# Second block of a transformer kernel: the index query and the small projection as two groups of 356 columns ahead of the query

## The reference, cut to what matters

```python
h = rmsnorm(x, norm_mix[layer])
proj = h @ w_in[layer]
qa, ka, va, qb, kb, vb, qi, ki, wi, ga, gb = jnp.split(proj, IN_OFFSETS, axis=-1)
...
qb = rope(qb.reshape(B, T, B_HEADS, HEAD_DIM), pos)
kb = rope(kb[:, :, None], pos)[:, :, 0]
qi = rope(qi.reshape(B, T, IDX_HEADS, IDX_DIM), pos)
ki = rope(ki[:, :, None], pos)[:, :, 0]
y_b = indexed_sparse_attention(qb, kb, vb, qi, ki, wi).reshape(B, T, D_B)
```

## Time and profile before

| what | before |
|---|---|
| median of 3 runs | 729.28 us (728.77 to 729.98) |
| the profiled execution | 728.69 us, of which the span from first to last instruction is 726.9 us |
| PE busy | 715.3 us, 98% of the span, 3776 matmuls |
| DVE, ACT, POOL busy | 515.6 us, 410.3 us, 25.0 us |
| chain that ended last | PE 90%, DVE 3%, ACT 2%, issue 2% |
| granted TensorE clock, mean | 0.999 |

### The profile page before, as it was taken

The page is one execution under the profiler, slowest core; times in us unless marked ns, Lnnn a source line. Parts: engine busy times, 40 slices in busy tenths (PEclk is TensorE's granted clock), DMA queues, the critical chain, the costliest instruction groups (busy, mean ns, idle before and its releaser), DMA issues.

```text
span 726.9 us, 9709 instructions
## 1 busy us (share of the span) xinstructions
PE 715.3 (98%) x3776; PEld 575.7 (79%) x3776; DVE 515.6 (71%) x908; ACT 410.3 (56%) x693; POOL 25.0 (3%) x44
## 2 busy tenths in 40 slices
PE   7999999999999999999999999999999999999996
PEld 5678885578888888888888777778888888888885
DVE  4689999897665866747898799766856455545544
ACT  4397658986754564456546676675465444344432
POOL 1030012001000000000100000000000000000000
PEclk9999999999999999999999999999999999999999
DMA  9994939517656576643558334443376556555511
GB/s 367 414 366 158 387 102 365 205 59 261 210 185 230 202 273 233 231 174 115 161 177 301 131 117 130 158 177 116 116 232 231 174 186 206 187 175 173 174 58 59
DMA packets 72717, 144.90 MB, mean 199 GB/s; under 512 B 4112, under 2 KB 27664, under 8 KB 71648
## 3 DMA queue, kind: packets, MB, share of 16 engines
q1 hardware_dynamic: 70864, 138.98, 54.9%
q0 software_dynamic: 1520, 5.03, 2.0%
q10 hardware_dynamic: 288, 0.27, 0.1%
HBM read 143.22 MB, written 1.05 MB: 198 GB/s over the span
## 4 chain that ended last, share of the span: by engine, by line
PE 90%; DVE 3%; ACT 2%; issue 2%; DMA 1%; POOL 0%; SPq 0%; POOLq 0%; DVEq 0%
PE bank L433 22%; PE bank L435 22%; PE bank L434 22%; PE bank L757 5%; PE bank L415 5%; PE bank L755 3%; DMA WX<-in_w_ada 1%; DVE WL L1543 1%; PE bank L509 1%; PE bank L452 1%; PE bank L473 1%; PE bank L512 1%; PE bank L515 1%; PE bank L889 1%; PE bank L911 1%
## 5 line engine op out<-in xcount | busy, mean ns | idle before, releaser
L1543 DVE TENSOR_TENSOR WL<-W,WH 128x1024 fp32r<-128x1024 f32 (+2 forms) x222 | 249.6, 1170 | 36.0 <-ACT WH L1042 35.8
L1042 ACT ACTIVATE WH<-W 128x1024 fp32r<-128x1024 f32 (+2 forms) x222 | 211.9, 1011 | 51.0 <-DMA W<-in_w_mlp 35.7
L433 PE MATMUL bank<-WH,AHL 128*128 128x512 f32 (+1 forms) x480 | 189.0, 394 | 0.7 <-DVE WL L1543 0.4
L435 PE MATMUL bank<-WH,AHL 128*128 128x512 f32 (+1 forms) x480 | 185.4, 386 | 0.0
L434 PE MATMUL bank<-WL,AHL 128*128 128x512 f32 (+1 forms) x480 | 185.2, 386 | 0.0
L433 PEld LDWEIGHTS bank<-WH,AHL 128*128 128x128 f32 x480 | 90.2, 188 | 22.1 <-issue 4.0
L435 PEld LDWEIGHTS bank<-WH,AHL 128*128 128x128 f32 x480 | 90.1, 188 | 18.6
L434 PEld LDWEIGHTS bank<-WL,AHL 128*128 128x128 f32 x480 | 90.3, 188 | 16.9
L433 PE MATMUL bank<-WH,HH 128*128 128x512 f32 (+1 forms) x218 | 84.9, 390 | 0.0
L435 PE MATMUL bank<-WH,HL 128*128 128x512 f32 (+1 forms) x218 | 84.5, 388 | 0.0
L434 PE MATMUL bank<-WL,HH 128*128 128x512 f32 (+1 forms) x218 | 84.4, 387 | 0.0
(11 more groups left out here) (276 smaller groups left out, 853.0 us busy)
## 6 DMA issues: line engine op xcount, KB each, us to landing
W<-in_w_mlp SPq DMA_DIRECT2D x32, 1024.0 KB, 5.5
W<-in_w_in SPq DMA_DIRECT2D x24, 1024.0 KB, 5.8
W<-in_w_gate SPq DMA_DIRECT2D x22, 512.0 KB, 4.0
W<-in_w_up SPq DMA_DIRECT2D x22, 512.0 KB, 5.1
W<-in_w_down SPq DMA_DIRECT2D x11, 1024.0 KB, 5.0
W<-in_w_ada SPq DMA_DIRECT2D x10, 1024.0 KB, 7.9
WX<-in_w_ada SPq DMA_DIRECT2D x10, 1024.0 KB, 10.7
W<-in_w_out SPq DMA_DIRECT2D x8, 1024.0 KB, 5.1
```

The lines of the kernel that those rows point to most:

```text
L433: e.matmul(po, hs, wh[:, k, c0:c0 + cw], start=first and k == 0, stop=False)
L435: ins = e.matmul(po, ls, wh[:, k, c0:c0 + cw], start=False, stop=last and k == unit.nk - 1)
L1042: e.activation(m.WH[unit.slot][:, c], m.W32[unit.slot][:, c], ACT.Copy).then_inc(S["w_hi"], 1)
L1543: e.tensor_tensor(m.WL[unit.slot][:, c], m.W32[unit.slot][:, c], m.WH[unit.slot][:, c].bitcast(F32), ALU.subtract).then_inc(S["w_lo"], 1)
```

## The change

It regroups the 712 columns of qi and s and puts them ahead of qb. The unit "qi" now holds the first 356 columns of qi; the unit "s" holds the other 156 columns of qi and the 200 small columns, loaded in three pieces. Both take 356 columns. The slots stay in sequence: qi has W_0 and W_1 as before, s now W_4 and W_5, qb now W_2 and W_3. In `first2` PE runs qi, s, qb, and the turn of token block 1's norm stands in the middle of qb(0) and not behind it. ACT takes s's bank out in two copies (156 columns to raw, 200 to small), and the order of ACT's copies and DVE's rotations follows. On ACT the two high halves of W_5 no longer stand together between the second and the third sum of squares: one is there, the other between the third and the fourth. The matmuls' count stays.

```diff
-    two("qi", "w_in_2", 2176, True, "qi_mm", (3, 4))
+    two("qi", "w_in_2", 2176, True, "qi_mm", (3, 4), 356)
+    for i in range(2):
+        add("s", "w_in_2", 4 * i, 4, [("w_in_2", 2532, 156), ("w_in_2", 2048, 128), ("w_in_2", 2688, 72)], True, ("s_mm", 3 + i))
     two("qb", "w_in_2", 1536, True, "p2_mm", (3, 4))
-    for i in range(2):
-        add("s", "w_in_2", 4 * i, 4, [("w_in_2", 2048, 128), ("w_in_2", 2688, 72)], True, ("s_mm", 3 + i))
...
     def first2(tb):
-        product(by["qi"], m.AH, m.AL, tb, 4 + tb, "qi_mm", n_ready(1, tb))
-        frees(4 + tb, ("p2_out", 3 * tb + 1))
-        product(by["qb"], m.AH, m.AL, tb, tb, "p2_mm", n_ready(1, tb))
-        frees(tb, ("p2_out", 3 * tb + 2))
-        if tb == 0:
-            norm_turn(3, 1)
-        product(by["s"], m.AH, m.AL, tb, 2 + tb, "s_mm", n_ready(1, tb), 200)
-        frees(2 + tb, ("p2_out", 3 * tb + 3))
+        product(by["qi"], m.AH, m.AL, tb, 4 + tb, "qi_mm", n_ready(1, tb), 356)
+        frees(4 + tb, ("p2_out", 4 * tb + 1))
+        product(by["s"], m.AH, m.AL, tb, 2 + tb, "s_mm", n_ready(1, tb), 356)
+        frees(2 + tb, ("p2_out", 4 * tb + 3))
+        product(by["qb"], m.AH, m.AL, tb, tb, "p2_mm", n_ready(1, tb), 512, None if tb else lambda: norm_turn(3, 1))
+        frees(tb, ("p2_out", 4 * tb + 4))
...
-    def between(tb, mid):
+    def between(tb):
         i = 8 + 4 * tb
+        halves = high_halves(tb)
         for n in range(2):
             for j in range(2):
                 w.wait_ge(S["btw"], 8 * tb + 3 * n + 2 + j)
                 square(i + 2 * n + j, m.X[:, tb, 512 * n:512 * n + 512], m.S1[:, tb, 512 * n:512 * n + 512])
-            hi(mid[n])
+                if n != j:
+                    next(halves, None)
+        for _ in halves:
+            pass
...
     w.wait_ge(S["m2_mm"], 64)
     hi(2)
-    raw_out(0, "qi_mm", 2, 4, 0, 1.0)
+    index_out(0)
+    small_out(0)
+    norm_features(3, 1, m.mix, None)
     raw_out(1, "p2_mm", 2, 0, 0, 0.125)
-    norm_features(3, 1, m.mix, None)
-    small_out(0)
-    raw_out(0, "qi_mm", 4, 5, 1, 1.0)
+    hi()
+    index_out(1)
+    hi()
+    small_out(1)
     hi()
     raw_out(1, "p2_mm", 4, 1, 1, 0.125)
     hi()
-    small_out(1)
-    hi(2)
...
-    projected(1, 0, 0)
-    projected(2, 1, 0)
+    projected(2, 0, 0)
     small2(0)
-    projected(3, 0, 1)
+    projected(4, 1, 0)
     lo()
-    projected(4, 1, 1)
+    projected(5, 0, 1)
     lo()
     small2(1)
     features2(2, two(m.qiT, 1))
-    lo(2)
-    projected(7, 0, 0)
-    projected(7, 0, 1)
+    lo()
+    projected(7, 1, 1)
+    lo()
+    projected(9, 0, 0)
+    projected(9, 0, 1)
```

More of the change, by code:

```diff
@@ L848, in qa @@
         product(by["qa"], m.AH, m.AL, tb, 2 + tb, "p2_mm", n_ready(1, tb), 512, between)
-        frees(2 + tb, ("p2_out", tb + 7))
+        frees(2 + tb, ("p2_out", tb + 9))
     qa(0, lambda: p2_turn(m.rr[0], 5, (("p2_act", 1), ("p2_dve", 1))))
     for i in (1, 0):
-        w.wait_ge(S["p2_r"], 8)
+        w.wait_ge(S["p2_r"], 7)
         b = turn([(tb, m.skk[i][:, tb, :]) for tb in range(2)], "p2_turned")
@@ L859, in tensor_program @@
         product(by["ka"], m.AH, m.AL, tb, tb, "p2_mm", n_ready(1, tb))
-        frees(tb, ("p2_out", tb + 9))
+        frees(tb, ("p2_out", tb + 11))
         dots(4 * tb)
@@ L866, in tensor_program @@
                 (lambda: p2_turn(m.rr[1], 12, (("p2_act", 6), ("p2_act", 7)))) if tb else None)
-        frees(2 + tb, ("p2_out", tb + 11))
+        frees(2 + tb, ("p2_out", tb + 13))
     def gate(p, half):
@@ L904, in pv2 @@
         w.wait_ge(S["pt2"], 2 * p + 2)
-        w.wait_ge(S["p2_out"], 12)
+        w.wait_ge(S["p2_out"], 14)
         take(2)
@@ L1334, in between, with index_out @@
                 square(i + 2 * n + j, m.X[:, tb, 512 * n:512 * n + 512], m.S1[:, tb, 512 * n:512 * n + 512])
-            hi(mid[n])
+                if n != j:
+                    next(halves, None)
+        for _ in halves:
+            pass
         w.wait_ge(S["rstd"], 8 + 2 * tb)
         copy(m.S1[:, tb, 512:1024], m.X[:, tb, 512:1024], "nscale_act", m.stat[:, 47 + 2 * tb:48 + 2 * tb])
-    between(0, (0, 0))
+    between(0)
     norm_features(2, 0, m.mix, None)
     hi()
-    between(1, (1, 0))
+    between(1)
+    def index_out(tb):
+        from_bank("qi_mm", 2 + 2 * tb, m.raw[0][:, tb, 0:356], 4 + tb, slice(0, 356), "p2_out")
     def small_out(tb):
-        from_bank("s_mm", 2 + 2 * tb, m.small[:, tb, :], 2 + tb, slice(0, 200), "p2_out")
+        from_bank("s_mm", 2 + 2 * tb, m.raw[0][:, tb, 356:512], 2 + tb, slice(0, 156), "p2_out")
+        from_bank("s_mm", 2 + 2 * tb, m.small[:, tb, :], 2 + tb, slice(156, 356), "p2_out")
     def raw_out(i, sem, value, bk, tb, scale):
@@ L2058, in small2 @@
     def small2(tb):
-        w.wait_ge(S["p2_out"], 3 * tb + 3)
+        w.wait_ge(S["p2_out"], 4 * tb + 3)
         for i, c0 in ((0, 0), (1, 128)):
             rope2(m.skk[i][:, tb, :], m.small[:, tb, c0:c0 + 64].unsqueeze(1).to_broadcast([128, 2, 64]), 2, tb)
-    projected(1, 0, 0)
-    projected(2, 1, 0)
+    projected(2, 0, 0)
     small2(0)
-    projected(3, 0, 1)
+    projected(4, 1, 0)
     lo()
-    projected(4, 1, 1)
+    projected(5, 0, 1)
     lo()
@@ L2091, in vector_program @@
     for tb in range(2):
-        projected(9, 1, tb)
+        projected(11, 1, tb)
     features2(8, two(m.qaT, 1))
```

## The result

The change is slower: its median is 732.79 us (4 runs, 731.92 to 733.10) against 729.34 us of the kernel before beside it (728.77 to 729.98), a ratio of 1.0045 [1.0028, 1.0062]. That is 3.45 us, where 1.83 were forecast, and the time lies 0.4 us above the range. Run again later in five more executions (experiment 5), it took 730.80 against 728.87. The reason for the two figures is the main finding.

A forecast was written before the change was run, and what follows sets the result against it. PE was taken to bound the kernel, busy for 98% of the span. PE 2.2 us late at qi(1), less 0.39 us from token block 1's columns, gave 729.28 + 1.83 = 731.1 us; range 729.8 to 732.4.

The forecast's parts named there:

- The wait and its price: PE ahead of qb(0): stands 2.6 us until W_2's first low half at 365.8, so qi(1) starts 2.2 us late.
- The steps of the norm: ACT and DVE, token block 1: third square at 358.50, closing sums 360.71, scaling 362.81 instead of 364.60, 1.8 us earlier.
- The columns: PE's qi and s: 0.161 us per matmul of 356 columns, a gain of 0.39 us per token block.
- rival (d): Behind the stand ahead of qb(0), TensorE falls to 1.2 GHz for W_2's 12 matmuls: 2.7 us more, 733.8; chance 0.03.
- Rival (c): Turn of qi in qa(0): W_1 lands over 1.7 us late and PE waits, about 732.3 us; chance 0.09.
- what was costed at nothing: Loads in three pieces, ACT's extra copies and DVE's new order: no cost, with 1.7 us of cover at qi's turn in qa(0).

The follow-up runs named there:

- experiment 5: The change itself, unaltered, in five more executions: median 730.80 us, 1.0034 against the kernel before.
- Experiment 4: The change with W_2's high halves on ACT and low halves on DVE made ahead of the scaling of token block 1's norm: 728.92 us, 0.9996.
- experiment 6: The kernel before with one added wait, PE starting s(0) only when ACT has made the last of token block 1's features: 732.25 us, 1.0047.
- experiments 1 and 7: The change with 13 and 6 spare 356-column matmuls respectively in PE's wait ahead of qb(0): 731.04 us (1.0026) and 730.50 us (1.0023).
- experiment 3: The change with both high halves of W_5 together again between the second and third square on ACT: 731.77 us, 1.0041.

## Why the prediction was wrong, and where it was right

**The wait and its price: right.** The forecast was +1.83; with the clock up the change costs +1.74 by the trace up to the turn of qi, +1.86 with the skk turn, and 731.04 - 729.13 = +1.91, 730.50 - 728.87 = +1.63 with the stand filled; the three executions of the change under 731 lie at +1.63 to +1.93. The releaser (W_2's first low half), the place (ahead of qb(0)) and the time (365.8) are as worked out; the stand is 2.3 us by the prediction's count (365.80 less 363.35 + 0.16) and not 2.6, since s(0) ended 0.3 later. Experiment 4 shows that this wait carries the loss.

**The steps of the norm: right in sum, by two errors that cancel.** The third square was put at 358.50 and the closing sums at 360.71; they came at 358.80 and 361.04, with a start of qi(0) 0.23 later than the sum assumed. From the closing sums to the scaling 2.10 us were carried over from before; it took 1.78 (361.04 to 362.82). So the scaling stood at 362.82 where 362.81 was said.

**The columns: right.** 0.161 us for 356 columns; (381.53 - 374.03) / 46 = 0.163. The line through 256 and 512 was the better guide than the 200-column row above it. The Trainium skill (TensorE: Matmul & The Clock Gate, Back-to-back issue gap) has N / 2.4 GHz plus 2.5 ns for a full-rate matmul, an estimate of 0.151 for 356 columns; the trace is above that here as it was for 512, and the measurement decides.

**The step that failed: rival (d), the clock, with a chance of 0.03 and 2.7 us.** It came in five or six of nine executions and cost 1.58 to 1.6 us. The mechanism had been named, with its place; both the chance and the size were off, and the sum and the range (up to 732.4) left it out.
The chance rested on one stretch of before, a clock of 1.00 while PE did nothing for 2.76 us, and that reading was wrong. The trace has no record of the clock before 5.89 us, and a window without a record shows 1.00. PE's own rows tell more (windows with the columns as above):

```profile
2.76 5.32 PE L495 MATMUL bank<-ones 128*128 128x128 f32 x32 [2.76 <-POOL ones L353]
...
4.00:6.00 2.00, 2.00 (x11) 2.00 (x11) 0.33 (x2) 1.67 (x4) 0.07 (x1) 1.00 1.01 401
6.00:8.00 2.00, 2.00 (x19) 1.88 (x17) 0.81 (x2) 0.62 (x2) 1.04 (x2) 1.00 0.98 399
```

The same matmuls of 128 columns are 0.213 us apart up to 5.9 and 0.112 from there on, a ratio of 1.9, as 0.427 to 0.2266 for 512 columns at the two levels of the clock. So the trace of before did have a stretch at the slow distance, behind a time in which PE had done nothing. That is no proof of a fall behind a stand in the middle of the program, but it is no ground for 0.03 either. And experiment 5 shows that even the same stand, in the same place, goes either way, so no single row could have excluded a fall.
The size took all 12 matmuls of W_2 at half rate. In the trace the half rate lasts from about 366.0 to 369.4, eight distances of 0.43 and one of 0.32, and the clock comes back inside the group: W_2's 12 matmuls took 370.23 - 365.80 = 4.43 us instead of the 2.82 worked out, 1.61 more.
The Trainium skill (TensorE: Matmul & The Clock Gate, HAM oscillation — how this bites in real kernels) describes such a pattern in another kernel, waits between groups of matmuls that put the clock back so that the next group starts at half rate. The first profile of the change agrees with it (0.44 between the first two matmuls behind the stand); in experiment 6 the clock fell too, but 1.3 us into the next group; the second profile of the change, with the same stand, has no fall.

**A second wait: half right.** Rival (c) put it at the turn of qi, if W_1 landed over 1.7 us late. There is none at that turn, but half of the cover was gone: with the clock up DVE's last rotation of qi(1) ends at 386.57 + 0.69 = 387.26, against 388.02, a cover of 0.8 us where 1.7 had been worked out. The late term is the load of W_1, which lets ACT begin W_1's high halves at 382.94 and not at 382; s(1)'s copies on ACT and the rotation on DVE stand behind them (the change with the clock up, ACT and DVE):

```profile
382.94 2.01 ACT L1040 ACTIVATE WH<-W 128x1024 fp32r<-128x1024 f32 x2 [1.64 <-DMA W<-in_w_in]
...
385.17 0.69 DVE L1559 TENSOR_TENSOR rr<-raw,rope 128x512 f32<-128x512 f32 x1 [2.77 <-ACT raw L1048]
```

And what was costed at nothing meets PE one turn later. The third transpose of the skk turn starts 0.05 us after DVE's copy of qiT has ended (393.24 + 0.68 with the clock down), which frees its bank. The copy stands behind two low halves and the small rotations, as before; but that work began 4.6 us ahead of the turn of qi before (381.74) and 2.9 ahead of it here (385.17). That is 0.12 to 0.30 us. It follows W_1: where ACT began W_1's halves 5.7 and 5.5 us ahead of the turn of qi (experiments 1 and 7), the skk turn has 0.35 to the next matmul as before; at 5.1 (the change, clock up) it has 0.47, and at 4.9 (clock down, experiments 3 and 4) 0.62 to 0.66.

**Open.** What decides between the two outcomes of the change is not settled. Stands of 2.12 to 2.13 us did both; the one of 2.35 ended in a fall five times in five; behind the one of 1.15, with the stand filled and with it taken away, no execution took the time of a fall (nine, ten and eleven of them). PE's list alone does not decide it: in the two profiles of the change, with the same program and the first matmul at 2.75 or 2.76, the matmuls of line 495 are 0.213 us apart up to 5.7 us in one and up to 7.6 in the other. In experiment 3 the execution of 732.72 us has a mean clock of 0.998, as the faster ones, and its extra microsecond is not explained. That mean is a rough sign: it leaves out the stretch at the program's start that has no record, and counts one behind PE's last product (before: 0.55 over the last 0.9 us), so the groups are told apart here by their times.

## What to carry to other kernels

Where a unit of weights is moved ahead in PE's order, compare its halves with the work that covers the step in front of them: here 10.9 us of matmuls covered the norm before and 7.7 after, while what stood behind the norm grew from halves of 400 to halves of 1024 columns. On a kernel in which PE is busy all the time, price a new stand of two microseconds or more with and without a fall of the clock behind it (here 1.8 and 3.4 us), and give the fall a real chance; one trace in which the clock stayed up doesn't exclude it. Read the level of the clock from the distance between matmuls of the same width too: a granted clock of 1.00 in a window can mean that nothing was recorded there. And take a change apart: its small part, one half of a weight between two squares, was worth 0.94 us by itself and was hidden under the loss of the large one.

## What was not expected of the hardware

Behind a stand of 2.1 us between matmuls TensorE's granted clock went from 2.4 to 1.2 GHz in some executions of one kernel and not in others. The fall does not come at a fixed point after the stand: in the change the first matmul after it is already slow (0.44 to the next), in experiment 6 PE ran 1.3 us at full rate (369.14 to about 370.5, 0.11 between matmuls) and only then fell. At half rate 512 columns are 0.427 us apart, 1.9 times their distance at full rate, and 200 columns 0.213 ((372.99 - 370.86) / 10), 1.9 times their 0.1118. And work that computes nothing can be cheaper than standing: with thirteen or six spare matmuls in a wait that stayed as long (qb(0) starts 11.24 and 11.25 us behind qi(0)), none of 19 executions took more than 731.67 us, while five of the nine of the change took 732.3 or more. It buys nothing where the clock stays up: those executions of the change took 730.50 to 730.80 us, as the filled ones.
